# Paged cache loads laid out as 32 partitions of four tokens each, in a one-core hybrid decoder step

## Chip, core and metric

The kernel runs on one core of one Trainium2 chip. The metric is the device time of one execution in microseconds (us).

## What is computed

One inference step of a single decoder layer, for a prompt of 256 tokens and for 8 sample sequences of 8 new tokens each (320 token columns in all). The layer has three sub-layers: a SwiGLU feed-forward block, a mixer of two head groups (sparse block attention "MoBA" and gated linear attention "GLA"), and a second SwiGLU block, each with a modulation before it and a layer norm after it. All data are float32. What the change touches is the block attention of the samples over their cached past:

```
k_past = cache_k[layer, page_table]              # 8 sequences x 16 pages x 128 tokens x 8 heads x 64
kmean  = mean of k_past over blocks of 256 tokens
idx    = top 3 of the 8 blocks by q . kmean, for each query and head
s_sel  = q . k of the chosen blocks / 8,   s_own = q . k_new / 8
p      = softmax over the chosen blocks and the own tokens
o      = p . v of the chosen blocks + p_own . v_new
```

A physical page is 128 tokens of 512 floats, so 256 KB that lie together in memory. The page table is data: the number of each page is read at run time. There are 8 x 16 pages of K and as many of V, 256 transfers and 67.1 MB in all.

## The kernel before

Every matrix product with a weight is made of three float32r products (high x high, high x low, low x high). ScalarE rounds each 1 MB weight tile to its high part (`high`), VectorE forms the rest (`low`, L1743), and TensorE multiplies (`pair_slot`, L742, L743, L747). The order of work is fixed by hand: first the modulation vectors and the first feed-forward block, then twelve weight tiles of the mixer's input projection (MI), then the cache attention with GLA and prompt attention between its pieces, then four tiles of the mixer's output projection (MO), the second feed-forward block, and the last norm.

The stage of this change is the cache attention. SyncE issues its loads in a fixed list of 64 groups (`PAGE_GROUPS`, L160 to L204). A group is four pages of K or V of one sequence (1.05 MB). Each group has one of several buffers (`place_groups`): four in `ring`, which lies over the four weight buffers `raw`; one, named IN_H, in the halves of `pages_h` and `pages_l`; and for some time one in `M` and one in `W`. `load_pages` (L645) reads four page numbers, waits until the buffer's last user is done (`wait_used`), and issues four transfers (L666), one for each page. A page goes to 128 partitions, one token of 512 floats (2 KB) to each. After the list SyncE loads the last MO tiles and the weights of the second feed-forward block, through the same queue and partly into the same memory.

For a group of K, TensorE waits for the group (`wait_pages`, L971), and transposes each page in four pieces of 128 x 128 (`turn_keys`, L982). ScalarE (L1478) and VectorE (L2001) copy the four results to `kT`. After the groups of both sequences of a pair (index `i`, four steps `j` of 512 tokens), `scores` (L993) multiplies them with the queries into a bank of 512 columns: two blocks of 256 tokens. VectorE takes the sum and the maximum of each block (`block_values`, L2008 and L2010), ScalarE copies the bank to `prob` (L1486), and after four steps `choose` (L2021) ranks the blocks. ScalarE applies the exponential to one block at a time with that block's bias (`exps`, L1498). TensorE transposes the results (L1013), they are copied to `PT`, and `values` (L1031) multiplies them with the groups of V. In the code `PT[:, 4g+p]` belongs to the p-th quarter of the group that `wait_pages` returns. The last pieces of the list are V groups of the last pair; between them TensorE works on MO (`early_slot`, L798 to L803), and after them follow `late_slot` (L812) and the remaining MO tiles.

Of the kernel before, what the change touches and what calls it, by code (L numbers as in the profile page):

```python
# [23 lines left out]
I32 = mybir.dt.int32  # L24
ALU = mybir.AluOpType
ACT = mybir.ActivationFunctionType
X_AXIS = mybir.AxisListType.X


P = 128  # L30
# [1 line left out]
KT = D // P  # L32
S = 256
NB, T = 8, 8
NS = NB * T
# [5 lines left out]
HP = H // 2  # L41
# [7 lines left out]
BLK = 256  # L49
NBLK = PAST // BLK  # L50
# [157 lines left out]
IN_RING, IN_H, IN_M, IN_W = range(GROUPS), GROUPS, GROUPS + 1, GROUPS + 2  # L208
# [4 lines left out]
def place_groups():  # L213

    queue, last, buf, before = [(MI + x) % R for x in range(R)] + [IN_H], {}, [], []
    for n in range(len(PAGE_GROUPS)):
        if n in BEGIN_AT:
            queue.insert(0, BEGIN_AT[n])
        queue = [b for b in queue if n <= LAST_IN.get(b, n)]
        b = queue.pop(0)  # L220
        queue.append(b)
        buf.append(b)
        before.append(last.get(b))
        last[b] = n
    return buf, before, last


BUF, GROUP_BEFORE, LAST_GROUP = place_groups()
TURN_IN = [BUF[:n + 1].count(BUF[n]) for n in range(len(BUF))]
# [25 lines left out]
def dve_through(n):  # L255

    return n + 1 - act_through(n)
# [78 lines left out]
def layer_kernel(nc, a, o):  # L336
    ctx = ExitStack()
    with ctx:
        def sb(name, shape, dt=F32, where=ctx):
            return where.enter_context(nc.sbuf_tensor(name, shape, dt))  # L340

        def sem(name):
            return ctx.enter_context(nc.semaphore(name))
# [12 lines left out]
        ring = sb("ring", [P, RING, 512])  # L356
        kT = sb("kT", [P, 2, HP, 512])
        prob = sb("prob", [P, PAST])
# [3 lines left out]
        with ExitStack() as inputs:  # L362
            pages_h = sb("pages_h", [P, KT, N], F32, inputs)
            pages_l = sb("pages_l", [P, KT, N], F32, inputs)
# [43 lines left out]
        with ExitStack() as mixer:  # L408
            M = sb("M", [P, NCH, N], F32, mixer)
            W = sb("W", [P, WORK], F32, mixer)  # L410
            small = sb("small", [P, 192], F32, mixer)

        B = [ctx.enter_context(nc.psum_tensor(f"B{i}", [P, 512], F32)) for i in range(8)]
# [28 lines left out]
        def page_at(b, j):  # L442

            if b == IN_H:
                half = (pages_h, pages_l)[j // 2][:, HP:KT, :].rearrange("p c n -> p (c n)")
                return half[:, 512 * (j % 2):512 * (j % 2) + 512]
            if b == IN_M:
                return M[:, :, :].rearrange("p c n -> p (c n)")[:, 512 * j:512 * j + 512]
            if b == IN_W:
                return W[:, 512 * j:512 * j + 512]  # L450
            return ring[:, 4 * b + j, :]

        def late_out(k):
            return (B[OB], tb(("pick", NPAIR - 1)))[k][0:NS, 0:256]

        def tb(key):

            return B[BANK[FILL_AT[key]]][:, :]
# [3 lines left out]
        def cut(w):  # L462
# [25 lines left out]
        prob_own, PT_own, om = arow[:, 0, 0:P], arow[:, 0, P:2 * P], arow[:, 1, :]  # L488
# [3 lines left out]
        gate, rank, bmax, nbias, sums = (small[:, 0:8], small[:, 8:16], small[:, 16:25], small[:, 25:34],  # L492
                                         small[:, 34:43])
# [9 lines left out]
        page_landed = [sem(f"page_landed_{i}") for i in range(GROUPS + 3)]  # L503
# [5 lines left out]
        act_step, dve_step, pool_step = sem("act_step"), sem("dve_step"), sem("pool_step")  # L509
# [28 lines left out]
        o_hi, s_act, s_dve = sem("o_hi"), sem("s_act"), sem("s_dve")  # L538
# [34 lines left out]
        def split_through(n):  # L573

            return parts_before(n + 1)
# [5 lines left out]
        def _(sp):  # L581
# [6 lines left out]
            def wait_used(n):  # L588

                kind, i, g, bi = PAGE_GROUPS[n]  # L590
                if kind == "k":
                    sp.wait_ge(tp_filled, FILL_AT[("k", i, g, bi, 3)] + 1)
                else:
                    sp.wait_ge(v_used, v_index(i, bi, g) + 1)
# [50 lines left out]
            def load_pages(n):  # L645

                kind, i, g, bi = PAGE_GROUPS[n]
                cache = a["cache_k"] if kind == "k" else a["cache_v"]
                _, page = nc.values_load_multi_w_load_instructions(
                    pages[0:1, bass.ds((2 * i + bi) * NPAGE + 4 * g, 4)], engines=[mybir.EngineType.SP],  # L650
                    min_val=0, max_val=NPHYS - 1,
                    skip_runtime_bounds_check_because="a page table holds numbers of physical pages")
                b = BUF[n]
                if GROUP_BEFORE[n] is not None:
                    wait_used(GROUP_BEFORE[n])
                elif b == IN_H:
                    sp.wait_ge(used, MI + 12)
                elif b == IN_M:
                    sp.wait_ge(tp_filled, FILL_AT[("po", 3)] + 1)
                elif b == IN_W:  # L660
                    sp.wait_ge(stored, 4 * 16)
                    sp.wait_ge(tp_filled, FILL_AT[("go", 3)] + 1)
                else:
                    sp.wait_ge(lo_ready, split_through(MI + 8 + (b - MI) % R))
                for j in range(4):
                    sp.dma_start(page_at(b, j), cache[bass.ds(page[j], 1), :, :].rearrange("o s f -> s (o f)")  # L666
                                 ).then_inc(page_landed[b], 16)

            for k in range(4):
                load_ada(A1 + k)  # L670
# [44 lines left out]
            for n, (half, t) in enumerate(Y_GROUPS):  # L715
# [6 lines left out]
                dst = o["y_prompt"][t0:t0 + tn, fs] if t < 2 else o["y_sample"][:, fs]  # L722
# [6 lines left out]
        def _(pe):  # L729
# [76 lines left out]
            def late_slot(k):  # L806

                t = At(MO + k)
                vh, vl = split_view(wh, t.n0, "wide"), split_view(wl, t.n0, "wide")
                out = late_out(k)  # L810
                for c in range(HP):
                    pe.matmul(out, Hh[:, c, S:N], vh[:, c, :], start=(c == 0), stop=False)  # L812
                    pe.matmul(out, Hl[:, c, S:N], vh[:, c, :], start=False, stop=False)
                    m = pe.matmul(out, Hh[:, c, S:N], vl[:, c, :], start=False, stop=(c == HP - 1))
                m.then_inc(used, 1)
# [154 lines left out]

            def wait_pages(key):  # L971
                n = GROUP_AT[key]
                pe.wait_ge(page_landed[BUF[n]], 64 * TURN_IN[n])
                return [page_at(BUF[n], j) for j in range(4)]

            def turn_keys(i, j, bi):
# [397 lines left out]
        def _(act):  # L1374
            step = Steps(act, act_step)

            def act_(out, in_, func=ACT.Copy, **kw):
                return act.activation(out, in_, func, **kw)  # L1378
# [109 lines left out]
            def exps(i, lo, hi):  # L1488

                if lo == 0:  # L1490
                    act.wait_ge(bias_ready, i + 1)
                    act.wait_ge(own_ready, i + 1)
                    act.wait_ge(s_act, 4 * i + 4)
                    if i >= 1:
                        act.wait_ge(rinv_ready, i)
                for n in range(lo, hi):
                    v = prob[:, BLK * n:BLK * (n + 1)] if n < NBLK else prob_own[:, 0:NS]
                    act_(v, v, ACT.Exp, scale=HD ** -0.5, bias=nbias[:, n:n + 1],  # L1498
                         accum_out=sums[:, n:n + 1]).then_inc(exp_done, 1)

# [86 lines left out]
            for n in range(12):  # L1587
                act.wait_ge(used, MI + n + 1)
                c, b0 = 2 * MI_TILES[n], 2 * (n % 2)
# [17 lines left out]
                if n == 4:  # L1607
                    act.wait_ge(roped, 4)
                    act.wait_ge(q_zero, 1)
                    for hh in range(2):  # L1610
                        for bi in range(2):
                            rows = slice(HD * hh, HD * hh + HD)
# [42 lines left out]
            for i in range(NPAIR):  # L1655
                m0 = 4 * i + 3
                if i == 0:
# [19 lines left out]
                    continue  # L1677
                point(m0)
                exps(i, 0, 9)
                point(m0 + 1)  # L1680
                if i:
# [48 lines left out]
        def _(dve):  # L1730
# [15 lines left out]
            def strip_sum(pair):  # L1746
# [3 lines left out]
                at = 4 * PAIR_AT[pair]  # L1750
                dve.tensor_reduce(mod[:, at:at + 4, :], src, X_AXIS, ALU.add).then_inc(ada_sum, 1)

# [251 lines left out]
            def block_values(i, j):  # L2004

                dve.wait_ge(s_out, 2 * (4 * i + j) + 2)
                src = B[j % 2][:, :].rearrange("p (n k) -> p n k", n=2)
                dve.tensor_reduce(gate[:, 2 * j:2 * j + 2], src, X_AXIS, ALU.add).then_inc(dve_step, 1)  # L2008
                step.k += 1
                dve.tensor_reduce(bmax[:, 2 * j:2 * j + 2], src, X_AXIS, ALU.max).then_inc(s_dve, 1)  # L2010

            def own(i):

# [4 lines left out]
                dve.wait_ge(tp_dve, dve_through(n))  # L2018
                dve.tensor_reduce(bmax[:, NBLK:NBLK + 1], dst, X_AXIS, ALU.max).then_inc(own_ready, 1)

            def choose(i):  # L2021
# [9 lines left out]
                step(dve.tensor_tensor(wins, wins, ties, ALU.add))  # L2031
                step(dve.tensor_reduce(rank, wins, X_AXIS, ALU.add))
                step(dve.tensor_scalar(rank, rank, TOPK - 0.5, NEG, ALU.is_gt, ALU.mult))
                step(dve.tensor_tensor(bmax[:, 0:NBLK], bmax[:, 0:NBLK], rank, ALU.add))
                step(dve.tensor_reduce(mneg, bmax, X_AXIS, ALU.max))
                if i >= 1:
# [227 lines left out]
            for n in range(12):  # L2264
# [9 lines left out]
                else:  # L2274
                    for h in range(2):
                        dve.wait_ge(mi_sig, 2 * (n - 10) + h + 1)
                        c = 2 * MI_TILES[n] + h
# [265 lines left out]
```

## Time and profile before

| | us |
|---|---|
| median of 3 runs | 924.43 |
| lowest and highest | 923.56, 928.8 |
| the profiled execution's own time | 924.8 |
| its span in the trace | 923.0 |
| the stage from the fifth page group on (428 to 632) | 204 |

TensorE's mean granted clock over the span is 0.984 of full speed. In the rows below, TensorE work is "PE", its weight loads "PEld", VectorE "DVE", ScalarE "ACT", SyncE's own queue "SPq". The DMA share is the mean busy share of the core's 16 DMA engines, and can be read a little above 1 where a window cuts packets; GB/s is what they moved. "q1" is the queue of SyncE, "q10" that of ScalarE, "q0" that of GpSimd. The time to landing of a transfer runs from its issue to its last byte and contains the waiting behind earlier transfers.

### The profile page before, as it was taken

How to read it: one execution, taken by the hardware profiler on the slowest of the kernel's cores; microseconds unless marked ns; L12 is line 12 of the kernel's file. 1: busy time of each engine (PE TensorE's matmuls, PEld its weight loads, DVE VectorE, ACT ScalarE, POOL GpSimd, SP SyncE). 2: the span in 40 equal slices, each digit the busy share in tenths (PEclk: the TensorE clock that was granted, in tenths of full speed). 3: DMA queues.
4: the chain of work that ended last, by engine and by line, in shares of the span. 5: the costliest groups of instructions: out<-in, count | busy, mean ns of one | idle time of the engine just before them, and what ended most of it. 6: DMA issues, size and time to landing. Idle time of an engine off the chain costs nothing. (4 is left out here: it accounts for less than half of the span.)

```text
span 923.0 us, 17144 instructions
## 1 busy us (share of the span) xinstructions
PE 865.4 (94%) x6891; PEld 761.7 (83%) x6891; DVE 554.6 (60%) x882; ACT 353.2 (38%) x503; POOL 27.7 (3%) x32
## 2 busy tenths in 40 slices
PE   6999999999999899999879998888899999989994
PEld 2588898888999489998657877678699999989993
DVE  0645455446566589685865556663776765565556
ACT  1524233233433445454564435341343323323431
POOL 0000000000000000000000000000300000000002
PEclk9999999999999999999999999999999999999997
DMA  9999898897546853545959999998736555434521
GB/s 326 307 295 270 257 261 240 239 264 204 150 142 190 277 179 95 186 143 165 338 184 339 386 346 381 356 379 270 200 90 174 148 137 157 135 95 126 157 64 58
DMA packets 215173, 200.97 MB, mean 218 GB/s; under 512 B 9601, under 2 KB 161293, under 8 KB 214966
## 3 DMA queue, kind: packets, MB, share of 16 engines
q1 hardware_dynamic: 213700, 196.04, 68.4%
q0 software_dynamic: 704, 2.49, 0.7%
q10 hardware_dynamic: 690, 1.35, 0.5%
q8 instruction: 55, 0.90, 0.4%
q14 instruction: 24, 0.20, 0.1%
HBM read 196.04 MB, written 3.80 MB: 217 GB/s over the span
## 5 line engine op out<-in xcount | busy, mean ns | idle before, releaser
L1743 DVE TENSOR_TENSOR wl<-raw,wh 128x2048 fp32r<-128x2048 f32 x90 | 206.7, 2298 | 96.1 <-ACT wh L1378 95.8
L742 PE MATMUL B<-Hh,wh 128*128 128x320 f32 x864 | 258.8, 313 | 1.2 <-ACT wh L1378 1.2
L743 PE MATMUL B<-Hl,wh 128*128 128x320 f32 x864 | 255.0, 309 | 0.0
L1378 ACT ACTIVATE wh<-raw 128x2048 fp32r<-128x2048 f32 x90 | 172.2, 1913 | 147.2 <-PE B L747 98.0
L742 PEld LDWEIGHTS B<-Hh,wh 128*128 128x128 f32 x864 | 162.2, 188 | 11.5 <-issue 9.5
L743 PEld LDWEIGHTS B<-Hl,wh 128*128 128x128 f32 x864 | 162.3, 188 | 0.3
L747 PE MATMUL B<-Hh,wl 128*128 128x320 f32 x864 | 144.3, 309 | 0.0
L747 PEld LDWEIGHTS B<-Hh,wl 128*128 128x128 f32 x864 | 131.1, 188 | 0.0
L742 PE MATMUL B<-Gh,wh 128*128 128x320 f32 x352 | 104.5, 311 | 2.5 <-DVE Gl L1926 2.5
L743 PE MATMUL B<-Gl,wh 128*128 128x320 f32 x352 | 103.8, 309 | 0.0
L1378 ACT ACTIVATE sg<-B 128x320 f32<-128x320 f32 x46 | 20.1, 438 | 194.6 <-PE B L747 178.2
L1918 DVE TENSOR_TENSOR hf<-sg,B 128x320 f32<-128x320 f32 x44 | 21.4, 487 | 102.7 <-ACT sg L1378 102.7
L742 PEld LDWEIGHTS B<-Gh,wh 128*128 128x128 f32 x352 | 66.0, 188 | 2.7 <-DVE Gl L1926 2.7
L743 PEld LDWEIGHTS B<-Gl,wh 128*128 128x128 f32 x352 | 66.1, 188 | 0.0
L747 PE MATMUL B<-Gh,wl 128*128 128x320 f32 x352 | 56.8, 309 | 0.0
L982 PE MATMUL B<-cst,ring 128*128 128x128 f32 x368 | 48.3, 287 | 6.2 <-ACT kT L1378 3.4
L982 PEld LDWEIGHTS B<-cst,ring 128*128 128x128 f32 x368 | 42.6, 148 | 13.7 <-issue 6.6
L747 PEld LDWEIGHTS B<-Gh,wl 128*128 128x128 f32 x352 | 52.9, 188 | 0.0
L2001 DVE COPY kT<-B 128x512 f32<-128x512 f32 x62 | 41.2, 687 | 14.7 <-PE B L982 14.7
L1378 ACT ACTIVATE kT<-B 128x512 f32<-128x512 f32 x66 | 36.0, 605 | 12.1 <-PE B L982 12.1
L842 PE MATMUL B<-raw,cpk 128*32 128x512 f32 x288 | 40.0, 634 | 0.3 <-ACT cpk L1378 0.3
L1031 PE MATMUL B<-ring,PT 128*32 128x128 f32 x800 | 25.1, 274 | 7.0 <-DVE PT L2057 3.7
(279 smaller groups left out, 952.9 us busy)
## 6 DMA issues: line engine op xcount, KB each, us to landing
raw<-in_w_ffn_in SPq DMA_DIRECT2D x88, 512.0 KB, 6.3
raw<-in_w_ada SPq DMA_DIRECT2D x72, 512.0 KB, 4.9
ring<-in_cache_v SPq DMA_DIRECT2D x100, 256.0 KB, 5.0
ring<-in_cache_k SPq DMA_DIRECT2D x92, 256.0 KB, 4.8
raw<-in_w_ffn_out SPq DMA_DIRECT2D x32, 384.0 KB, 3.4
raw<-in_w_mix_in SPq DMA_DIRECT2D x24, 512.0 KB, 4.9
raw<-in_w_ffn_out SPq DMA_DIRECT2D x32, 320.0 KB, 4.0
pages_h<-in_cache_k SPq DMA_DIRECT2D x14, 256.0 KB, 4.5
```

The costliest lines, as they stand in the source:

```text
L742: pe.matmul(out, w, xh[k], start=start and k == 0, stop=False)
L743: pe.matmul(out, w, xl[k], start=False, stop=False)
L747: m = pe.matmul(out, w, xh[k], start=False, stop=stop and k == last)
L842: m = pe.matmul(B[ada_bank(pair)][32 * k:32 * k + 32, :], cpk[:, 4 * half + k, :], v[:, k, :], start=(half == 0), stop=(half == 1))
L982: m = pe.transpose(bank[:, c * P:(c + 1) * P], at[p][:, c * P:(c + 1) * P], ident)
L1031: m = pe.matmul(out[32 * c:32 * c + 32, :], PT[:, 4 * g + p, 32 * c:32 * c + 32], at[p][:, c * P:(c + 1) * P], start=(g == 0 and p == 0), ...
L1378: return act.activation(out, in_, func, **kw)
L1743: dve.tensor_tensor(dst, raw_view(n), f32(wh[:, wbuf(n), :]), ALU.subtract).then_inc(lo_ready, 1)
L1918: step(dve.tensor_tensor(hf[:, j, :], sg[:, j, :], B[2 * j][:, 0:N], ALU.mult))
L2001: dve.tensor_copy(kT[:, bi, :, p * P:(p + 1) * P], tb(key).rearrange("p (c s) -> p c s", c=HP)).then_inc(tp_dve, 1)
```

## The change

Each page is now written to 32 partitions: page j of a group goes to partitions 32j to 32j+31, and partition 32j+r gets tokens 4r to 4r+3, 8 KB that lie together in memory. A page is still one transfer of 256 KB, four to a group. Only in the buffer IN_H, whose two halves lie in two tensors, a page is two transfers of 4 KB rows, so a group is eight, and the count that is waited for is 128 in place of 64.

The x-th quarter of a group (512 floats of each partition) now holds tokens 4r+x of all four pages, and no more one page. The transposes, scores and value products run as before on these quarters, since keys and values of a step are permuted alike. A block of 256 tokens is no more 256 neighbouring columns of the scores but four strips of 64 columns, 128 columns apart. So the sums and maxima (L2007 to L2010) and the exponentials (L1497) go over strips, on the same number of elements.

```diff
+        def page_rows(b, rows):
+
+            if b == IN_H:
+                halves = [v[:, HP:KT, :].rearrange("p c n -> p (c n)") for v in (pages_h, pages_l)]
+                return [(halves[x][rows, 0:1024], 1024 * x) for x in range(2)]
+            if b == IN_M:
+                return [(M[:, :, :].rearrange("p c n -> p (c n)")[rows, 0:2048], 0)]
+            if b == IN_W:
+                return [(W[rows, 0:2048], 0)]
+            return [(ring[:, 4 * b:4 * b + 4, :].rearrange("p j f -> p (j f)")[rows, :], 0)]
...
                 for j in range(4):
-                    sp.dma_start(page_at(b, j), cache[bass.ds(page[j], 1), :, :].rearrange("o s f -> s (o f)")
-                                 ).then_inc(page_landed[b], 16)
+                    rows = slice(32 * j, 32 * j + 32)
+                    src = cache[bass.ds(page[j], 1), :, :].rearrange("o (r x) f -> r (o x f)", x=4)
+                    for dst, lo in page_rows(b, rows):
+                        sp.dma_start(dst, src[:, lo:lo + dst.shape[1]]).then_inc(page_landed[b], 16)
...
-                pe.wait_ge(page_landed[BUF[n]], 64 * TURN_IN[n])
+                pe.wait_ge(page_landed[BUF[n]], (128 if BUF[n] == IN_H else 64) * TURN_IN[n])
...
-                    v = prob[:, BLK * n:BLK * (n + 1)] if n < NBLK else prob_own[:, 0:NS]
+                    v = prob_own[:, 0:NS]
+                    if n < NBLK:
+                        four = prob[:, 512 * (n // 2):512 * (n // 2 + 1)].rearrange("p (x b k) -> p b x k", x=4, b=2)
+                        v = four[:, n % 2]
...
-                src = B[j % 2][:, :].rearrange("p (n k) -> p n k", n=2)
-                dve.tensor_reduce(gate[:, 2 * j:2 * j + 2], src, X_AXIS, ALU.add).then_inc(dve_step, 1)
+                src = B[j % 2][:, :].rearrange("p (x n k) -> p n x k", x=4, n=2)
+                dve.tensor_reduce(gate[:, 2 * j:2 * j + 2], src, XY_AXES, ALU.add).then_inc(dve_step, 1)
                 step.k += 1
-                dve.tensor_reduce(bmax[:, 2 * j:2 * j + 2], src, X_AXIS, ALU.max).then_inc(s_dve, 1)
+                dve.tensor_reduce(bmax[:, 2 * j:2 * j + 2], src, XY_AXES, ALU.max).then_inc(s_dve, 1)
```

## Rows read from the trace of the kernel before

**Rows 1.** The page's first part: busy time of each engine

```profile
PE 865.4 (94%) x6891; PEld 761.7 (83%) x6891; DVE 554.6 (60%) x882; ACT 353.2 (38%) x503; POOL 27.7 (3%) x32
```

**Rows 2.** Windows of the cache attention: stretch, its length, engines' busy us, PEclk, DMA share, GB/s

```profile
428.00:485.00 57.00, 47.05 (x427) 33.26 (x426) 40.29 (x105) 32.34 (x88) 0.00 (x0) 0.98 0.77 262
485.00:545.00 60.00, 57.31 (x781) 45.96 (x781) 31.45 (x68) 26.10 (x67) 0.00 (x0) 0.96 0.99 355
545.00:600.00 55.00, 49.84 (x626) 37.62 (x628) 34.92 (x80) 25.68 (x54) 0.72 (x1) 0.97 1.03 369
600.00:632.30 32.30, 29.08 (x505) 26.44 (x504) 15.43 (x36) 10.55 (x24) 1.17 (x1) 1.00 0.95 344
```

**Rows 3.** The chain that ended last, 598 to 660: start, us, what

```profile
613.64 9.00 DMA ring<-in_cache_v
```

**Rows 4.** Waits, 425 to 640: us in total, times, longest us

```profile
PEld B L1031 <- DMA ring<-in_cache_v: 3.7, 3, 1.9
...
PE B L1031 <- DMA ring<-in_cache_v: 3.0, 2, 1.6
```

**Rows 5.** SyncE's queue in order of time: start, us, what

```profile
389.24 28.79 SPq L666 DMA_DIRECT2D ring<-in_cache_k  x16
427.95 0.85 SPq L666 DMA_DIRECT2D pages_h<-in_cache_k  x2
...
541.78 7.50 SPq L666 DMA_DIRECT2D ring<-in_cache_v  x12
```

**Rows 6.** DMA queues, 428 to 632: packets, MB, share of 16 engines

```profile
q1 hardware_dynamic: 36672, 65.03, 89.8%
q10 hardware_dynamic: 528, 1.05, 1.8%
q0 software_dynamic: 320, 1.18, 1.5%
```

**Rows 7.** DMA rate in 40 slices of 0.3 us, 620 to 632

```profile
GB/s 389 396 376 396 376 403 369 417 369 396 382 382 382 389 389 382 389 382 396 382 444 362 362 376 369 396 376 369 369 246 191 178 109 41 0 0 0 0 0 0
```

**Rows 8.** Windows of half a us around the load of `x_sample` (64 partitions); columns as in rows 2

```profile
17.00:17.50 0.50, 0.50 (x3) 0.15 (x1) 0.00 (x0) 0.00 (x0) 0.00 (x0) 1.00 1.06 402
17.50:18.00 0.50, 0.50 (x6) 0.10 (x8) 0.00 (x0) 0.00 (x0) 0.00 (x0) 1.00 1.17 205
18.00:18.50 0.50, 0.50 (x8) 0.06 (x8) 0.00 (x0) 0.00 (x0) 0.00 (x0) 1.00 1.00 176
18.50:19.00 0.50, 0.50 (x9) 0.10 (x2) 0.00 (x0) 0.00 (x0) 0.00 (x0) 1.00 0.95 213
19.00:19.50 0.50, 0.50 (x5) 0.50 (x6) 0.00 (x0) 0.00 (x0) 0.00 (x0) 1.00 0.98 246
```

**Rows 9.** The issue of `x_sample`: start, us; and KB, us to landing

```profile
8.29 0.58 SPq L675 DMA_DIRECT2D xn<-in_x_sample  x1
...
xn<-in_x_sample SPq DMA_DIRECT2D x1, 256.0 KB, 11.5
```

**Rows 10.** DMA packets of 60 to 66.5, with the 1316.5 KB of `cst`, 128 partitions

```profile
DMA packets 2610, 2.29 MB, mean 353 GB/s; under 512 B 1104, under 2 KB 2379, under 8 KB 2481
```

**Rows 11.** Windows while `cst` lands; columns as in rows 2

```profile
60.00:61.00 1.00, 1.00 (x9) 1.00 (x8) 0.63 (x1) 0.82 (x2) 0.00 (x0) 1.00 1.24 504
61.00:62.00 1.00, 1.00 (x9) 1.00 (x8) 1.00 (x1) 0.00 (x0) 0.00 (x0) 1.00 0.92 377
62.00:63.00 1.00, 1.00 (x8) 0.86 (x6) 0.66 (x1) 0.00 (x0) 0.00 (x0) 1.00 1.06 453
```

**Rows 12.** Groups of instructions, 425 to 640: busy us, mean ns of one

```profile
L1378 ACT ACTIVATE kT<-B 128x512 f32<-128x512 f32 x66 | 36.0, 605 | 12.1 <-PE B L982 12.1
...
L1378 ACT ACTIVATE prob<-prob,small 128x256 f32<-128x256 f32 x32 | 15.8, 496 | 4.4 <-DVE small L2039 4.4
...
L2010 DVE TENSOR_REDUCE small<-B 128x2 f32<-128x512 f32 x16 | 10.9, 682 | 0.0
L1378 ACT ACTIVATE prob<-B 128x512 f32<-128x512 f32 x16 | 9.6, 598 | 53.8 <-DVE small L2010 53.8
```

More of the change, by code:

```diff
@@ L26 @@
 ACT = mybir.ActivationFunctionType
-X_AXIS = mybir.AxisListType.X
+X_AXIS, XY_AXES = mybir.AxisListType.X, mybir.AxisListType.XY
 P = 128
```

## The prediction, made before the changed kernel was run

> **What bounds the kernel now.** The page's busy times come first [rows 1]: TensorE is busy for 94% of the span, so elsewhere than in the stage of this change the kernel is its. I then read the windows of the cache attention [rows 2]. The reader should see two things there. TensorE is busy 80 to 95% of each stretch, and from 485 us on the 16 DMA engines are as full as they get (share 0.95 to 1.03) at 344 to 369 GB/s. The stage runs on two limits that are nearly equal. The waits say how much of it the transfers take now: TensorE's value products wait 3.7 and 3.0 us for V groups [rows 4], and the chain passes once over a V transfer, for 9.00 us [rows 3]. So faster transfers can give a few us at most, while slower ones have next to no cover: the engines already have a full queue for 147 of 204 us.
>
> The queue's own order [rows 5]: the first 16 transfers (4 groups) are issued by 418 us, the first of the other 60 groups at 428 us. Rows 7 show the last page bytes landing at about 629.9 us. The 60 groups therefore have 201.9 us.
>
> **The change, part by part.**
>
> *Bytes and packets.* The 60 groups are 62.9 MB (60 x 4 x 262144 bytes). With two MO tiles (2.1 MB) this is the 65.03 MB of SyncE's queue in the stretch [rows 6]. Other queues add 2.2 MB. Before the change none of this is slower than the engines can take; the question is the rate at which 8 KB rows go to 32 partitions.
>
> *Row size alone.* The load of `cst` has rows of 10.5 KB to 128 partitions. Of its time, 129 packets are not under 8 KB [rows 10], about one for each partition, so a long row travels as one packet. Its three windows average 445 GB/s, with lumps since a packet counts at one end [rows 11]; the 2 KB pages make 382 to 396 [rows 7]. Long rows by themselves are worth 15% at most.
>
> *Partition span.* One load of the trace writes few partitions: `x_sample`, 64 partitions of 4 KB rows, issued at 8.3 us and landed 11.5 us later, at 19.8 [rows 9]. With it in flight the rate falls from 402 to 205, 176, 213 and 246 GB/s, while the engines' busy share stays at 0.95 to 1.17 [rows 8]. The engines are held, not idle: about half of the path into the on-chip memory is used. Here the rows are long, too, and that doesn't help. Page j of the new layout goes to partitions 32j to 32j+31, so each transfer spans even fewer partitions. Pages 0 and 1 fill the same half that `x_sample` fills, pages 2 and 3 the other. All engines take their shares of the transfers in the order of issue, so they should all be in the same half at the same time. I take the mean of the four windows, 210 GB/s; the bounds are their ends, 176 and 246.
>
> This is the SBUF port map of the Trainium skill (SBUF — State Buffer, section on the DMA port swizzle and on issuing two DMAs to hit both halves): partitions 0 to 31 reach 8 of 16 ports, as do 0 to 63, and two transfers in flight, one to each half, came out only 6% faster than one. The trace agrees on the 64-partition load (rows 8) and doesn't show two alternating halves. With the page's 189 GB/s for 32 partitions the sum below would be about 1067 us, with its asymptote of 218 about 1023.
>
> *The sum.* 62.9 MB at 210 GB/s is 299.6 us. The two MO tiles and the other queues' 2.2 MB, 4.3 MB at 386, add 11.2. The stream starts at 428 us and ends at 738.8 in place of 629.9: +108.9 us. It stays unbroken, since five to seven buffers are in play, a group takes 5.0 us to arrive and TensorE's work for a group is 183.3 us / 60, or 3.1 us [rows 2]. What comes after the last V group is the same as before: the next MO tile still waits for the ring's last reader (`wait_free`, L596). 924.8 + 108.9 = 1033.7, say 1034 us. The profiled execution's time is 0.4 us over the median of the three runs.
> At 176 GB/s the stream lasts 368.6 us and the kernel takes 1091 us; at 246 it lasts 266.9 and the kernel takes 990.
>
> *More issues.* IN_H takes 9 of the 64 groups, so 36 transfers more. Two issues take 0.85 us, and 12 take 7.50 us without a break, so one is 0.5 to 0.6 us of the queue [rows 5]: 18 to 22 us in all, 2 us for each such group. With 5 us of transfer per group this hides completely. Without that cover (fast transfers), a group in IN_H needs 4 to 5 us of issue for at most 2.7 us of transfer.
>
> *Strips on VectorE and ScalarE.* Same elements, same count: 32 reductions of 0.68 us, and 32 exponentials of 0.50 us [rows 12]. The rows bound what strips cost: the copy to `kT`, which writes four strips of 128, takes 605 ns and the plain one to `prob` 598. I take 0 and as an upper bound 1 us on the chain; if reductions doubled (22 us) they'd still lie beside the waits for pages. TensorE idles more in the stage, so its clock may fall from the 0.96 to 1.00 of rows 2; up to 3 us after the last group would go to that, at best 0.
>
> **The rivals.**
>
> *A, long rows win: faster or unchanged.* The engines come apart in time: some work in pages 0 and 1 while others are in 2 and 3, both halves stay busy, and each page takes up to 15% less. For it: nothing ties the engines to each other inside a full queue, and foreign packets disturb them singly. Against it: a lead of one engine over its neighbour must grow to two whole pages before both halves are used, and nothing in rows 8 drives it; every time the queue runs dry the lead is lost. The price is what TensorE waits for pages now, 6.7 us [rows 4] of which I give it half: 921 us. The point from which it decides: 62.9 MB in 201.9 - 11.2 us, so 330 GB/s; above it the end doesn't move later. The Trainium skill (Perfetto Trace Analysis, DMA Optimizations) speaks for this side: batching rows of 2 KB to 4 or 8 KB can improve throughput where the kernel is bound by DMA. The trace agrees for 128 partitions (rows 11) and shows nothing for 32.
>
> *B, SyncE's queue takes the gain back.* If A holds for the transfers, the 36 added issues, 18 us, fall on a queue that already needs 2.5 us a group, as much as the transfer. Then the result is about 924 us: no change.
>
> *C, half apart.* Engines separate partly, the rate is 246 to 330 GB/s: 925 to 990 us, middle 957.
>
> *D, the change doesn't do what it says*, because 8 KB rows are cut to smaller packets. Rows 10 speak against it, and the partitions would still be 32; the time would be that of my forecast.
>
> **How the numbers follow.** Forecast (with D): 0.68, 990 to 1091 us by itself. C: 0.12. A: 0.13. B: 0.07. What a measurement of this kernel can tell from no change is about 0.5%. Slower is forecast and C, 0.80; faster 0.13; same 0.07. The range leaves A and B out, 2 in 10, and takes in C nearly whole and the bounds of the rate: 935 to 1091. The predicted time is that of the likeliest case.
>
> **What would show it.** In the changed profile: the DMA share stays near 1 from 430 us on while GB/s reads about 210; the page stage ends at about 740 us; value products and key transposes (L1031, L982 of before) wait for page transfers for 80 us or more in total; the time to landing of a page rises from 5 us to over 10; the page's packets of 8 KB number 7040 (220 pages of 32) beside 2304 of 4 KB; the reductions stay at 0.68 us. I'm wrong if the rate in that stage is at or above 330 GB/s: then A or B is read from the gaps between SyncE's issues. A rate near 210 with the time unchanged would mean that the stage had slack which rows 2 don't show.

## The result, and the profile after

The changed kernel takes 998.92 us (median of 5 runs, 993.04 to 1002.15) against 923.56 us before in the same comparison (5 runs). The ratio is 1.0806, with a 95% interval of 1.0755 to 1.0857: the change makes the kernel 8% slower. The profiled execution took 993.04 us, the fastest of the five.

The page of the changed kernel, parts 1 and 2 (40 slices of 24.8 us) and the page transfers of part 6 (KB each, median us to landing):

```profile
PE 893.2 (90%) x6891; PEld 782.1 (79%) x6891; DVE 555.3 (56%) x882; ACT 354.7 (36%) x503; POOL 27.8 (3%) x32
...
PEclk9999999999999999999977997967999999999997
DMA  9999889975568545679999999999755555534531
GB/s 329 296 307 257 253 255 255 252 218 146 148 177 276 187 127 156 155 159 232 231 233 239 245 251 316 319 220 272 227 127 145 153 147 151 155 90 118 146 88 54
...
ring<-in_cache_v SPq DMA_DIRECT2D x100, 256.0 KB, 14.0
ring<-in_cache_k SPq DMA_DIRECT2D x92, 256.0 KB, 14.7
```

From the 19th to the 28th slice the DMA engines are busy for 90% or more, but slices 19 to 24 read 231 to 251 GB/s, where full engines moved 355 to 369 before [rows 2]. A page now needs 14 us to land; before it was 5.0 us in `ring`. VectorE and ScalarE work as long as before in total [rows 1]: 555 and 355 us.

The windows of the page stage, to be held against [rows 2]:

```profile
430.00:485.00 55.00, 44.48 (x375) 30.96 (x377) 38.54 (x99) 30.72 (x82) 0.00 (x0) 0.97 1.02 229
485.00:540.00 55.00, 41.22 (x485) 33.22 (x484) 19.39 (x50) 18.62 (x51) 0.00 (x0) 0.72 1.03 235
540.00:600.00 60.00, 43.20 (x566) 31.41 (x566) 21.34 (x44) 22.33 (x48) 0.72 (x1) 0.93 1.03 253
600.00:650.00 50.00, 43.09 (x468) 32.40 (x463) 31.51 (x74) 17.94 (x42) 0.00 (x0) 0.88 1.03 308
650.00:700.00 50.00, 37.49 (x413) 32.60 (x409) 10.95 (x18) 5.13 (x5) 1.17 (x1) 0.70 0.92 225
```

The share stays at 1.02 to 1.03 and the rate starts at 229, two thirds of the 355 to 369 of before. It is not constant: it climbs to 308 and falls again. The waits of TensorE for pages, which were 3.7 and 3.0 us [rows 4] (us, times, longest; 425 to 720):

```profile
PEld B L1044 <- DMA ring<-in_cache_v: 32.8, 14, 6.0
PE B L1044 <- DMA ring<-in_cache_v: 28.6, 13, 5.7
...
PEld B L995 <- DMA ring<-in_cache_k: 13.3, 7, 3.6
...
PE B L995 <- DMA ring<-in_cache_k: 9.5, 5, 3.3
```

L1044 and L995 are L1031 and L982 of before. SyncE's queue around the last pages, and the first load behind them (start, us):

```profile
640.72 13.39 SPq L680 DMA_DIRECT2D ring<-in_cache_v  x12
657.48 0.95 SPq L626 DMA_DIRECT2D W<-in_w_mix_out  x2
658.95 30.36 SPq L680 DMA_DIRECT2D ring<-in_cache_v  x20
700.68 3.29 SPq L626 DMA_DIRECT2D raw<-in_w_mix_out  x4
```

The same load of `raw` was issued at 632.29 us before. It is 68.4 us late, and the span grew by 68.1 us (923.0 to 991.1). So the whole difference comes from the page stage; after it the two kernels take the same time.

### The profile page after: what moved, and what is told of

It reads as the page before. It is cut to its first block, busy times and chain, and to the rows that moved or that the text cites. A ratio compares the mean times of both kernels' runs of the same rounds, so it can differ in the third digit from the quotient of the medians.

```text
span 991.1 us, 17252 instructions
## 1 busy us (share of the span) xinstructions
PE 893.2 (90%) x6891; PEld 782.1 (79%) x6891; DVE 555.3 (56%) x882; ACT 354.7 (36%) x503; POOL 27.8 (3%) x32
## 2 busy tenths in 40 slices
DMA packets 192325, 200.98 MB, mean 203 GB/s; under 512 B 10177, under 2 KB 161869, under 8 KB 185078
## 4 chain that ended last, share of the span: by engine, by line
PE 73%; DMA 16%; SPq 4%; DVE 4%; issue 2%; ACT 1%; POOL 0%; POOLq 0%; ACTq 0%; DVEq 0%
PE B L755 18%; PE B L756 18%; PE B L760 18%; DMA ring<-in_cache_v 7%; SPq L680 4%; PE B L855 3%; DMA ring<-in_cache_k 3%; PE B L995 2%; DMA M<-in_cache_v 2%; PE B L1044 2%; DMA W<-in_cache_v 2%; PE B L878 1%; PE B L863 1%; PE B L773 1%; PE B L783 1%
## 5 line engine op out<-in xcount | busy, mean ns | idle before, releaser
L755 PEld LDWEIGHTS B<-Hh,wh 128*128 128x128 f32 x864 | 162.2, 188 | 11.2 <-issue 9.5
L995 PE MATMUL B<-cst,ring 128*128 128x128 f32 x368 | 49.4, 291 | 15.3 <-DMA ring<-in_cache_k 9.5
L1044 PE MATMUL B<-ring,PT 128*32 128x128 f32 x800 | 33.9, 326 | 32.4 <-DMA ring<-in_cache_v 28.6
L995 PEld LDWEIGHTS B<-cst,ring 128*128 128x128 f32 x368 | 43.5, 150 | 23.0 <-DMA ring<-in_cache_k 13.3
L1044 PEld LDWEIGHTS B<-ring,PT 128*32 128x32 f32 x800 | 25.3, 129 | 39.2 <-DMA ring<-in_cache_v 32.8
```

The costliest lines, as they stand in the source:

```text
L755: pe.matmul(out, w, xh[k], start=start and k == 0, stop=False)
L995: m = pe.transpose(bank[:, c * P:(c + 1) * P], at[p][:, c * P:(c + 1) * P], ident)
L1044: m = pe.matmul(out[32 * c:32 * c + 32, :], PT[:, 4 * g + p, 32 * c:32 * c + 32], at[p][:, c * P:(c + 1) * P], start=(g == 0 and p == 0), ...
```

## The experiments

The theory, T1: a transfer that writes only partitions 0 to 63, or only 64 to 127, has half of the path into the on-chip memory. If the engines take their shares in order, all of them crowd into one half and then into the other. The rivals: T2, 8 KB packets are themselves slow; T3, the strips on VectorE and ScalarE cost the time; and, tried later, that the small number of rows in a transfer, the width of its span, or the number of transfers is what counts. Each comparison has its own runs of the kernel before, with medians of 924.55 to 924.61 us. Where no ratio stands the spread of the runs is given. Executions of one kernel whose transfers stay in one half scatter by 0.9 to 2.6% (E6: 980 to 1005 us), so two such kernels are told apart only where the difference is larger, or where the ratios to the kernel before have separate intervals. Each rate comes from one trace of one execution.

**E1, strips only.** The loads of before (and the count of 64 that is waited for) with the new reductions and exponentials.

```diff
                 for j in range(4):
-                    rows = slice(32 * j, 32 * j + 32)
-                    src = cache[bass.ds(page[j], 1), :, :].rearrange("o (r x) f -> r (o x f)", x=4)
-                    for dst, lo in page_rows(b, rows):
-                        sp.dma_start(dst, src[:, lo:lo + dst.shape[1]]).then_inc(page_landed[b], 16)
+                    sp.dma_start(page_at(b, j), cache[bass.ds(page[j], 1), :, :].rearrange("o s f -> s (o f)")
+                                 ).then_inc(page_landed[b], 16)
...
```

> The pages are loaded as before the change (128 partitions, 2 KB rows, 256 transfers); only the sums, maxima and exponentials go over strips. The blocks that are summed and weighted are then mixed from other tokens, so the sample attention's values differ; the work is the same. Theory T1 (the loads to 32 partitions hold the engines in one half of the path) and T2 (8 KB packets are slow) both expect the time of before, 924 us within 5, reductions at 0.68 to 0.70 us and exponentials at 0.50. Theory T3 (the strips cost the time) expects 990 to 1000.

Measured: 926.07 us, ratio 1.0021 (0.9998 to 1.0043). Its groups of instructions (busy us, mean ns):

```profile
L1389 ACT ACTIVATE prob<-prob,small 128x256 f32<-128x256 f32 x32 | 15.8, 495 | 5.4 <-DVE small L2053 5.4
L2024 DVE TENSOR_REDUCE small<-B 128x2 f32<-128x512 f32 x16 | 10.9, 681 | 0.0
```

Both are what they were [rows 12], to 1 ns. Strips of 64 columns cost nothing that these runs can tell. T3 is out.

**E2, short rows to 32 partitions.** Partition 32j+r gets tokens r, r+32, r+64 and r+96, so packets have 2 KB again.

```diff
-                    src = cache[bass.ds(page[j], 1), :, :].rearrange("o (r x) f -> r (o x f)", x=4)
+                    src = cache[bass.ds(page[j], 1), :, :].rearrange("o (x r) f -> r (o x) f", x=4)
...
-                        sp.dma_start(dst, src[:, lo:lo + dst.shape[1]]).then_inc(page_landed[b], 16)
+                        w = dst.shape[1]
+                        sp.dma_start(dst.rearrange("p (x f) -> p x f", f=512), src[:, lo // 512:(lo + w) // 512, :]
+                                     ).then_inc(page_landed[b], 16)
```

> As the changed kernel, page j to partitions 32j to 32j+31, but partition r gets tokens r, r+32, r+64, r+96, so every packet is 2 KB. T1 expects the slow kernel: 990 to 1010 us, about 230 GB/s from 430 to 540 us. T2 expects 924 to 930 and 380 GB/s where the queue is full.

Measured: 1010.05 us (4 runs, 994 to 1014). Two windows of the stage:

```profile
485.00:540.00 55.00, 38.04 (x469) 30.04 (x469) 19.22 (x51) 17.86 (x50) 0.00 (x0) 0.75 1.08 222
540.00:600.00 60.00, 43.82 (x510) 32.52 (x510) 22.68 (x46) 17.17 (x40) 0.72 (x1) 0.91 1.08 222
```

The packets of before, with the span of the change, are as slow as the change: the fastest of the four runs took 994 us, the median lies at the upper edge of what T1 expected, and the trace is of the slowest. T2 expected 380 GB/s and is out.

**E3, long rows to all partitions.** A group is one transfer of 128 rows of 8 KB. The kernel leaves out the page table and reads four neighbouring pages at a fixed place; the count that is waited for follows.

```diff
-                for j in range(4):
-                    rows = slice(32 * j, 32 * j + 32)
-                    src = cache[bass.ds(page[j], 1), :, :].rearrange("o (r x) f -> r (o x f)", x=4)
-                    for dst, lo in page_rows(b, rows):
-                        sp.dma_start(dst, src[:, lo:lo + dst.shape[1]]).then_inc(page_landed[b], 16)
+                at = 4 * (n % (NPHYS // 4))
+                src = cache[at:at + 4, :, :].rearrange("o (r x) f -> (o r) (x f)", x=4)
+                for dst, lo in page_rows(b, slice(0, P)):
+                    sp.dma_start(dst, src[:, lo:lo + dst.shape[1]]).then_inc(page_landed[b], 16)
...
```

> 8 KB rows to all 128 partitions: a group is one transfer of 1 MB from four neighbouring pages at a fixed place (the page table is left out, so the sample attention's values differ); two transfers for IN_H. 73 transfers in place of 292. T1 expects 400 GB/s or more where the queue is full, and 915 to 924 us, a few us under before. T2 expects 980 us or more with 230 to 250 GB/s.

Measured: 921.71 us, ratio 0.997 (0.9953 to 0.9987). The window 485 to 540, and its rate in 40 slices of 1.4 us, first of E3, then of the kernel before:

```profile
485.00:540.00 55.00, 52.96 (x714) 42.77 (x713) 29.57 (x65) 26.09 (x67) 0.00 (x0) 0.98 0.95 368
```

```profile
GB/s 214 411 203 369 402 223 381 423 387 304 375 191 310 411 417 420 405 405 396 435 417 405 441 399 429 411 417 402 423 420 417 423 429 399 441 405 435 268 101 152
GB/s 329 243 270 225 252 314 366 386 404 392 343 352 365 392 372 387 395 378 387 389 386 386 389 383 389 384 386 386 387 389 384 387 381 393 386 387 383 389 369 165
```

Where the queue is full (slices 14 to 37), 8 KB rows move at 396 to 441 GB/s, on average 417; the 2 KB rows of before at 372 to 395, on average 386. This fits the promise of long rows, about 8% of rate, and is worth 0.3% of the kernel. (E3 also has a quarter of the transfers and reads neighbouring pages, so the 8% isn't shown to be the rows' alone.) It is worth so little for a plain reason: the engines are no longer full all the time (share 0.95), and TensorE, busy for 52.96 of the 55 us, sets the pace.

**E4, the order 0, 2, 1, 3.** Neighbouring transfers go to different halves.

```diff
-                for j in range(4):
+                for j in (0, 2, 1, 3):
```

> As the changed kernel, but the pages of a group are issued in the order 0, 2, 1, 3, so that neighbouring transfers go to different halves. Under T1 an engine has to lead its neighbour by one page instead of two until both halves are in use, so the rate should rise sooner: 250 GB/s or more already between 430 and 540 us (changed kernel: 235), and 940 to 980 us. If the halves are not what matters (T2, T3), the order changes nothing: 993 to 1002 us.

Measured: 988.15 us, ratio 1.0711 (1.0647 to 1.0775).

**E7, runs of four pages in one half.**

```diff
-                for j in range(4):
+                for j in ((0, 1, 2, 3) if n % 2 == 0 else (2, 3, 0, 1)):
```

> As the changed kernel, but every second group issues its pages in the order 2, 3, 0, 1, so four transfers in a row go to the same half (two before, one in the order 0, 2, 1, 3). Under T1 with engines that come apart by chance, the lead that is needed doubles: the rate should stay near 230 GB/s or below it for longer (600 to 650 us: under 270 GB/s, changed kernel 308) and the time be 1005 to 1035 us. If the rise of the rate in the changed kernel has another cause, the order changes nothing: 993 to 1002 us.

Measured: 1028.28 us, ratio 1.1092 (1.1043 to 1.1141). The same four windows, first of E4, then of E7:

```profile
430.00:485.00 55.00, 45.55 (x390) 31.91 (x388) 39.14 (x102) 28.66 (x79) 0.00 (x0) 0.92 1.03 251
485.00:540.00 55.00, 44.34 (x574) 35.71 (x574) 24.11 (x55) 21.76 (x59) 0.00 (x0) 0.86 1.02 258
540.00:600.00 60.00, 49.69 (x555) 38.12 (x557) 26.35 (x63) 22.29 (x47) 0.72 (x1) 0.83 1.03 271
600.00:650.00 50.00, 37.77 (x431) 27.32 (x424) 24.27 (x57) 14.66 (x36) 0.00 (x0) 0.80 1.04 271
```

```profile
430.00:485.00 55.00, 46.77 (x372) 33.19 (x370) 35.02 (x90) 29.57 (x80) 0.00 (x0) 0.91 1.03 219
485.00:540.00 55.00, 35.21 (x449) 27.72 (x450) 20.18 (x55) 16.43 (x48) 0.00 (x0) 0.76 1.03 218
540.00:600.00 60.00, 44.99 (x484) 34.80 (x486) 22.08 (x44) 15.90 (x30) 0.00 (x0) 0.91 1.03 220
600.00:650.00 50.00, 33.42 (x341) 25.66 (x333) 21.61 (x48) 18.28 (x39) 0.73 (x1) 0.76 1.03 222
```

Bytes, packets and transfers are those of the changed kernel; only the order in which the halves are visited differs. Runs of one, two and four pages give 251, 229 and 219 GB/s in the first window, and 988, 999 and 1028 us. Of these times only the 1028 us stands clear; the intervals of E4 and of the changed kernel (1.0755 to 1.0857) overlap. With runs of four the rate stays at 218 to 222 for 220 us. This speaks for engines that come apart a little and gain from it when the runs are short. It is an argument and not shown: no run here looks at single engines, and E2, with runs of two pages in 2 KB packets, held 222 GB/s up to 600 us as well. My figure for E4, 940 to 980 us, was too hopeful; its median is 988. Alternating the halves page by page gives back about a seventh of what the change lost, by the medians, and not most of it.

**E6, a wider span in the same half.** Pages 0 and 1 to every second partition of 0 to 63, pages 2 and 3 likewise above.

```diff
-                    rows = slice(32 * j, 32 * j + 32)
+                    rows = slice(64 * (j // 2) + j % 2, 64 * (j // 2) + 64, 2)
```

> Page j goes to every second partition of one half: pages 0 and 1 to the even and odd partitions of 0 to 63, pages 2 and 3 to those of 64 to 127. The span of a transfer is doubled against the changed kernel but stays in one half. T1 expects no gain: 985 to 1010 us and about 230 GB/s up to 540 us. A theory T1c (the width of the span in partitions counts, 32 being a quarter of the path) expects clearly less than the changed kernel, 940 us or under.

Measured: 996.97 us (4 runs, 980 to 1005); 235 GB/s from 485 to 540, the figure of the changed kernel. The width inside a half doesn't count, and T1c is out.

**E5, a stepped span over both halves.** Page j to partitions j, j+4, j+8 and so on; the views of the strips follow.

```diff
-                    rows = slice(32 * j, 32 * j + 32)
+                    rows = slice(j, P, 4)
...
-                        four = prob[:, 512 * (n // 2):512 * (n // 2 + 1)].rearrange("p (x b k) -> p b x k", x=4, b=2)
+                        four = prob[:, 512 * (n // 2):512 * (n // 2 + 1)].rearrange("p (x b k) -> p b x k", x=P, b=2)
...
-                src = B[j % 2][:, :].rearrange("p (x n k) -> p n x k", x=4, n=2)
+                src = B[j % 2][:, :].rearrange("p (x n k) -> p n x k", x=P, n=2)
```

> Page j goes to partitions j, j+4, j+8 and so on to all parts of the 128, still 32 rows of 8 KB, one transfer a page and two in IN_H; a block is then 128 strips of 2 columns. T1 (what matters is which half of the partitions a transfer reaches) expects the rate of a full span, 370 GB/s or more where the queue is full, and 915 to 930 us, the strips of 2 columns and the 36 added issues being all that is left against before. A theory T1b (what matters is that a transfer has only 32 rows, two to each engine) expects 990 to 1010 us as in the changed kernel.

Measured: 950.67 us, ratio 1.0262 (1.0227 to 1.0297). Two thirds of the loss are gone, with 32 rows in a transfer as before, so T1b is out. But it isn't the 915 to 930 of T1. Two of its windows, and SyncE's queue (start, us):

```profile
485.00:540.00 55.00, 49.14 (x635) 40.43 (x637) 25.06 (x56) 22.71 (x59) 0.00 (x0) 0.88 0.83 274
636.00:645.00 9.00, 8.42 (x107) 8.01 (x106) 5.51 (x8) 2.94 (x3) 1.18 (x1) 0.88 1.03 385
```

```profile
553.05 0.47 SPq L680 DMA_DIRECT2D pages_h<-in_cache_v  x1
553.71 0.47 SPq L680 DMA_DIRECT2D pages_l<-in_cache_v  x1
...
559.16 8.77 SPq L680 DMA_DIRECT2D ring<-in_cache_v  x12
```

The DMA share is 0.83: the engines wait for work. An issue takes 0.47 us here and the next starts 0.66 us after the start of the first. From 488 to 600 us the queue issues or reads page numbers without a break, and from 425 to 630 us it waits for buffers for 20 us in all, against 46 in the kernel before. In the changed kernel an issue took 0.32 us and the next came after 0.50. So 60 groups with 36 added issues are 276 x 0.66 = 182 us plus the reads of page numbers, nearly the whole stage. That the stepped transfers themselves are not slow shows where the engines are full, in the second window: 385 GB/s, the rate of before. A bound that the change had covered shows once the transfers are quick: SyncE's own queue, my rival B in another place. The strips of 2 columns are not the cause; the reductions take 681 to 690 ns as before and the 32 exponentials 524 in place of 496, under 1 us together.

**E8 and E9, half the transfers, with and without both halves.** Two neighbouring pages, again at a fixed place and without the page table, make one transfer of 64 rows. E9 has `rows = slice(64 * j, 64 * j + 64)` in the line on `rows`. The counts that are waited for and the views of the strips follow, the same in both.

```diff
-                for j in range(4):
-                    rows = slice(32 * j, 32 * j + 32)
-                    src = cache[bass.ds(page[j], 1), :, :].rearrange("o (r x) f -> r (o x f)", x=4)
+                for j in range(2):
+                    rows = slice(j, P, 2)
+                    at = 4 * (n % (NPHYS // 4)) + 2 * j
+                    src = cache[at:at + 2, :, :].rearrange("o (r x) f -> (o r) (x f)", x=4)
...
```

> Full span with half the transfers of e5_step_4: a transfer is two neighbouring pages at a fixed place (the page table is left out, so the sample attention's values differ), 64 rows of 8 KB to every second one of all 128 partitions; two to a group, four in IN_H, 146 in all. If what e5_step_4 lost against before (26 us) is SyncE's queue, which there needs 0.65 us for each of 292 transfers, this gives 918 to 928 us and waits of SyncE's queue for buffers again. If it is the stepped rows, whose engines still meet in one half for a row at a time, this stays at 940 to 955 us.

> As e8_pairs_step_2, but the first transfer of a group goes to partitions 0 to 63 and the second to 64 to 127 (contiguous). Same bytes, same 8 KB rows, same 64 rows a transfer and same 146 transfers. T1 expects the slow kernel again, 985 to 1010 us with 225 to 240 GB/s up to 540 us, whatever the number of transfers. If the number of transfers or of rows in one is what makes the changed kernel slow, this comes to 930 us or under.

Measured: E8 923.43 us, ratio 0.9984 (0.9967 to 1.0); E9 993.07 us, ratio 1.0765 (1.0692 to 1.0839). One window of E8, from 485 to 600, and one of E9, from 430 to 540:

```profile
485.00:600.00 115.00, 107.64 (x1412) 83.44 (x1412) 66.20 (x146) 52.50 (x122) 0.73 (x1) 0.98 0.95 363
```

```profile
430.00:540.00 110.00, 83.06 (x862) 62.40 (x862) 58.04 (x149) 49.52 (x133) 0.00 (x0) 0.89 1.02 234
```

The two kernels differ in nothing but which 64 partitions a transfer writes: 70 us. That is the cleanest showing of T1. E8 also bears out that E5 lost its 26 us at the queue: stepped rows with half the issues are not slower than before, and SyncE's queue again waits for buffers, 120 us in all from 425 to 630 us. (E8 doubles the rows of a transfer too, so the queue is shown by E5's own trace more than by E8.) One thing is left open: no run wrote a contiguous range across partition 64, such as 32 to 95, so that the line between the halves lies just there is not shown.

None of these kernels that reads the page table beats the one before. E3 and E8 are 0.3 and 0.2% under it, at fixed places in the cache. With a page table that is read at run time this kernel gives each page a transfer of its own, and of the layouts tried with long rows E5 then costs least, 2.6% over the kernel before.

## Why the prediction was right, and where its size was off

- *The two near limits* [rows 2]: right. The engines had a full queue already from 485 us on, and a lower rate went to the end at once: 68 us.
- *Row size alone*: right in sign, and within the bound. I gave long rows 15% at most; E3 has about 8% in rate, with fewer and larger transfers besides, and 0.3% in time.
- *Partition span*: right that a transfer within one half is held to about half of the rate. E8 against E9 shows it, and E2 against the kernel before. The Trainium skill's port map (SBUF — State Buffer, the DMA port swizzle) agrees: its 8 of 16 ports for partitions 0 to 63 have an asymptote of 218 GB/s, and E7 holds 218 to 222.
- *The rate of 210 GB/s*: this is the term of the sum that was mis-sized. The stream ran from 427.6 to about 697 us, 269 us. Less the 11.2 us for other bytes, 62.9 MB went at 244 GB/s. The step behind it that failed is "they should all be in the same half at the same time". Where that comes nearest to holding, in E7, the sum is good: its load of `raw` is issued at 741.24 us, 109 us later than before, and the sum had +108.9. (The engines there move 218 to 222 GB/s, all queues together: 67.2 MB at 219 are 307 us, and the sum had 310.8. Why [rows 8] read a little lower is open; their windows may hold the edges of the load.) In the changed kernel, with runs of two pages, the rate starts at 229 and rises to 308, so the stream takes about 40 us less than the sum says.
- *How near it was*: 244 GB/s lies 2 under the 246 at which rival C begins, so the likeliest case, 990 to 1091 us, held by a narrow margin; the range on record, 935 to 1091, would have held either. The rate began as the forecast has it and ended as C has it, and I had no row for the rise. That its mean fell on the forecast's side is luck.
- *The stream stays unbroken*: right, the share is 1.02 to 1.03 up to 650 us; between 640 and 700 us the queue waits 9 us for buffers, and the engines stay full to 690.
- *More issues*: right that they hide under slow transfers. The 0.5 us an issue held. E5 shows what issues cost without that cover, at 0.66 us each.
- *Strips*: right, nothing (E1).
- *The clock*: TensorE's granted clock fell in the page stage, to 0.70 to 0.97 in the windows above, while the transfers set the pace. Busy time rose by 28 us [rows 1], but the work after the pages took no longer. I had allowed up to 3 us on the path and find none.
- *Waits*: I wrote 80 us or more for pages. The four rows above sum to 84 us, with TensorE and its weight loads each counted for the same waits. For TensorE's products alone it is 38 us, and 49 with the pages in `M`, `W` and `pages_l`. So the figure was too high for TensorE's products. They wait 46 us longer for pages than before and are busy 28 us longer, which together is about the 68 us of the loss.
- *Rival A* needed 330 GB/s; no window above reached it. *Rival D* is out: packets of 8 KB and over number 7247 (192325 less 185078) against 207 before, and the 7040 more are the number forecast.

## What to carry to other kernels

Before a load is reshaped for longer packets, look at which partitions each single transfer writes: in this kernel 8% of rate at most from 8 KB rows was paid for with a third of the rate from transfers that stay in one half of the partitions. Transfers to different halves do not make up for each other just because both are in the queue; a stepped set of partitions that reaches both halves keeps the full rate, if the issuing queue can afford 0.66 us a transfer. And where a stage has two limits close together, a gain in one is worth the distance to the other (0.3% here), a loss its whole size.

## What the runs showed of the hardware that was not expected

The rate of transfers that alternate between the halves isn't fixed. In the first window it falls with the number in a row that go to the same half: 251 GB/s for 256 KB, 222 to 229 for 512 KB (four kernels: E2, E6, E9 and the changed one), 219 for 1024 KB. And within one run it drifts: in the changed kernel from 229 to 308 in 220 us, then down to 203 in 8 us, with full engines throughout. Windows of 2 us around the fall:

```profile
642.00:644.00 2.00, 2.00 (x34) 1.55 (x37) 1.77 (x7) 1.24 (x2) 0.00 (x0) 1.00 1.07 307
644.00:646.00 2.00, 1.01 (x40) 0.75 (x36) 1.78 (x9) 1.35 (x4) 0.00 (x0) 1.00 1.02 256
646.00:648.00 2.00, 0.37 (x16) 0.10 (x4) 1.92 (x7) 2.00 (x9) 0.00 (x0) 1.00 1.01 214
648.00:650.00 2.00, 0.23 (x7) 0.21 (x10) 0.41 (x2) 1.55 (x8) 0.00 (x0) 0.89 1.12 203
650.00:652.00 2.00, 1.71 (x32) 1.17 (x24) 0.00 (x0) 0.00 (x0) 0.00 (x0) 0.50 1.08 195
```

What sets the engines apart and what brings them together again stays open; a load of an MO tile to all partitions had been issued at 638 us and may lie behind the fall, which no experiment tried. The last row shows a side effect: TensorE, busy for 0.37 and 0.23 us of the two windows of 2 us before it, is granted 0.50, the 1.2 GHz level, for its next products.

An issue takes longer for some sets of partitions: 0.32 us for 32 neighbouring ones and 0.47 for 32 stepped ones (E5, E6). With 64 partitions it is 0.47 us whether they are stepped or not (E8, E9), and with all 128 it is 0.33 (E3).
